# Router on the raw rows, half by half inside the output projection, and the order of splits and slots ahead of the first expert

## What is computed

```python
h = layer_norm(DN_ALPHA * h + y @ w_out, ln1_g, ln1_b)
h = layer_norm(DN_ALPHA * h + moe(h, w_router, b_router, w_gate, w_up, w_down), ln2_g, ln2_b)

def moe(...):                      # 16 experts in 4 groups, 2 chosen of the best group
    scores = sigmoid(h @ w_router)
    sel_score = scores + b_router
    ...
    for e in range(16):
        he = silu(h @ w_gate[e]) * (h @ w_up[e])
        y = y + combine[:, e:e + 1] * (he @ w_down[e])
```

## Time and profile before

| | |
|---|---|
| median of the runs | 886.03 us |
| profiled execution, own time | 888.82 us |
| its span, first to last instruction | 887.1 us |
| TensorE busy | 786.7 us (89%) |
| VectorE busy | 592.4 us (67%) |
| ScalarE busy | 430.9 us (49%) |
| GpSimd busy | 103.2 us (12%) |
| mean granted clock of TensorE | 0.951 of 2.4 GHz |

### The profile page before, as it was taken

One profiled execution on the slowest core, in us unless ns is written; L12 is line 12 of the kernel. 1 busy time (PEld: TensorE's weight loads), 2 busy tenths in 40 slices (PEclk: granted clock), 3 DMA queues, 4 the chain that ended last, 5 costly groups with the idle time before them and its releaser, 6 DMA issues.

```text
span 887.1 us, 10600 instructions
## 1 busy us (share of the span) xinstructions
PE 786.7 (89%) x3903; PEld 617.8 (70%) x3905; DVE 592.4 (67%) x793; ACT 430.9 (49%) x497; POOL 103.2 (12%) x115
## 2 busy tenths in 40 slices
PE   4499999999998999999999984799999999999920
PEld 2387898984676454688788873688888888888710
DVE  4805999793237654222356577799888988898838
ACT  5343343244532644422123121487778777877713
POOL 4630000000001000000000021211112111212012
PEclk9999999997999999999999985899999999999975
DMA  7644132400051300034323975499999999997143
GB/s 187 223 137 157 48 96 57 134 1 1 0 193 60 96 1 0 1 95 159 125 95 104 359 297 177 160 360 384 400 398 397 398 400 396 398 401 272 61 168 136
DMA packets 102644, 167.05 MB, mean 188 GB/s; under 512 B 18961, under 2 KB 39697, under 8 KB 102609
## 3 DMA queue, kind: packets, MB, share of 16 engines
q1 hardware_dynamic: 95024, 145.53, 46.3%
q0 software_dynamic: 4752, 13.11, 3.8%
q10 hardware_dynamic: 2832, 7.93, 2.3%
HBM read 153.38 MB, written 17.40 MB: 193 GB/s over the span
## 4 chain that ended last, share of the span: by engine, by line
PE 77%; DVE 11%; ACT 4%; issue 3%; DMA 2%; SPq 1%; POOL 1%; POOLq 0%; DVEq 0%; ACTq 0%
PE low L1011 14%; PE low L1012 14%; PE low L1013 14%; PE wide L1011 6%; PE wide L1013 6%; PE wide L1012 6%; PE wide L1365 2%; PE low L1188 1%; PE low L1260 1%; PE wide L1173 1%; ACT prob L844 1%; PE wide L1214 1%; PE low L1317 1%; PE low L1252 1%; PE low L1158 1%
## 5 line engine op out<-in xcount | busy, mean ns | idle before, releaser
L1731 DVE TENSOR_TENSOR m_lo<-m_raw,m_hi 128x2048 fp32r<-128x2048 f32 x95 | 214.9, 2290 | 28.4 <-ACT m_hi L890 25.4
L890 ACT ACTIVATE m_hi<-m_raw 128x2048 fp32r<-128x2048 f32 x95 | 179.1, 1917 | 25.6 <-PE low L1013 25.6
L1456 DVE TENSOR_TENSOR w_lo<-raw,w_hi 128x2048 fp32r<-128x2048 f32 x28 | 64.1, 2290 | 79.9 <-ACT w_hi L646 79.6
L1011 PE MATMUL low<-m_hi,xe_hi 128*128 128x512 f32 x256 | 103.7, 405 | 3.6 <-DVE xe_lo L1796 3.2
L1011 PE MATMUL low<-hT_hi,w_hi 128*128 128x512 f32 (+1 forms) x240 | 93.2, 388 | 10.7 <-issue 10.7
L1012 PE MATMUL low<-m_lo,xe_hi 128*128 128x512 f32 x256 | 100.4, 392 | 0.0
L1013 PE MATMUL low<-m_hi,xe_lo 128*128 128x512 f32 x256 | 100.4, 392 | 0.0
L1012 PE MATMUL low<-hT_lo,w_hi 128*128 128x512 f32 (+1 forms) x240 | 93.0, 387 | 0.0
L1013 PE MATMUL low<-hT_hi,w_lo 128*128 128x512 f32 (+1 forms) x240 | 92.3, 385 | 0.0
L646 ACT ACTIVATE w_hi<-raw 128x2048 fp32r<-128x2048 f32 x28 | 53.5, 1910 | 18.6 <-PE wide L1013 8.3
L1011 PEld LDWEIGHTS low<-hT_hi,w_hi 128*128 128x128 f32 x240 | 46.7, 195 | 20.9 <-issue 11.2
(11 more groups left out here) (337 smaller groups left out, 1524.7 us busy)
## 6 DMA issues: line engine op xcount, KB each, us to landing
m_raw<-in_w_gate SPq DMA_DIRECT2D x32, 1024.0 KB, 8.1
m_raw<-in_w_up SPq DMA_DIRECT2D x32, 1024.0 KB, 8.0
m_raw<-in_w_down SPq DMA_DIRECT2D x31, 1024.0 KB, 9.4
raw<-in_w_in SPq DMA_DIRECT2D x19, 1024.0 KB, 5.4
raw<-in_w_out SPq DMA_DIRECT2D x4, 1024.0 KB, 5.1
table_dram<-ftab ACTq DMA_DIRECT2D x8, 328.0 KB, 2.8
strips<-table_dram SPq DMA_DIRECT2D x8, 264.0 KB, 4.2
xn<-in_x SPq DMA_DIRECT2D x4, 512.0 KB, 5.2
```

The lines of the kernel that those rows point to most:

```text
L890: nc.scalar.activation(m_hi[n % MS][:, :], (m_spare if is_last(n, j) else m_raw[slot])[:, :], ACT.Copy).then_inc(q["m_hi_ready"], 1)
L1011: nc.tensor.matmul(outp, lh, rh, start=first, stop=False)
L1456: v.tensor_tensor(w_lo[:, u % SPL, :], raw[:, u % RAW, :], w_hi[:, u % SPL, :].bitcast(F32), ALU.subtract).then_inc(q["lo_ready"], 1)
L1731: v.tensor_tensor(m_lo[n % MS][:, :], (m_spare if is_last(n, j) else m_raw[n % MR])[:, :], m_hi[n % MS][:, :].bitcast(F32), ALU.subtract). ...
```

## The change

The logits of the router are linear in the normalized row but for the row's mean and deviation. So the router is applied to the raw rows (ALPHA·h + y @ w_out) as soon as a half of them is added. Its weights are multiplied by ln1_g and centred over the channels beforehand (`wrc`), so the mean drops out; the logits are then multiplied by `rstd1` and ln1_b's part (`rbias`) is added. The preparation stands early in the kernel: three small loads on SP behind units 0 and 1, four VectorE operations behind `split_lo(1)`, one matmul with ones, two VectorE operations ahead of `split_lo(3)`. Transposes and router are cut into halves of four blocks and put between the parts of half 1 of the output projection; the transposes wait for `z_added`, not for the finished h1, and VectorE waits for the transpose before it centres a row in place. The logits are put together on VectorE in tile 3. Behind the first lists the order of splits and slots changes on VectorE and TensorE.

```diff
@@ SP
             load(0)
             load(1)
+            sp.dma_start(wr[:, :, :], a["w_router"].rearrange("(c p) n -> p c n", p=P)).then_inc(q["wr_loaded"], 16)
+            sp.dma_start(ln1g[:, :], a["ln1_g"][0].rearrange("(c p) -> p c", p=P), allow_slow_non_contiguous=True).then_inc(q["wr_loaded"], 16)
+            sp.dma_start(ln1b[:, :], a["ln1_b"][0].rearrange("(c p) -> p c", p=P), allow_slow_non_contiguous=True).then_inc(q["wr_loaded"], 16)
             for i in range(CONV):
...
-            sp.dma_start(wr[:, :, :], a["w_router"].rearrange("(c p) n -> p c n", p=P)).then_inc(q["late_consts"], 16)
@@ GpSimd
+            step(nc.gpsimd.memset(ones_f[:, :], 1.0))
@@ ScalarE
+            for k in range(TT + 2):
+                turned_out(k)
             store_h1(0)
+            act.wait_ge(q["h1t_used"], 1)
+            nc.scalar.activation(lpart[:, :, :], bank[7][:, 0:TT * NE].rearrange("p (i x) -> p i x", i=TT), ACT.Copy).then_inc(q["part_out"], 1)
             store_h1(1)
-            turned_out(0)
-            turned_out(1)
+            turned_out(TT + 2)
+            store_h1(2)
+            turned_out(TT + 3)
             act.wait_ge(q["z_part"], 4 * TT)
-            store_h1(2)
-            turned_out(2)
             m_split_hi(0)
+            act.wait_ge(q["logit_ready"], 1)
+            nc.scalar.activation(tmp_r[0][:, :, :], logit[:, :, :], ACT.Sigmoid).then_inc(q["scores_ready"], 1)
+            store_h1(3)
             m_split_hi(1)
...
@@ TensorE, early
+            pe.wait_ge(q["wsum_ready"], 1)
+            nc.tensor.matmul(bank[2][:, 480:480 + 2 * NE], ones_f[:, :], wsum[:, :], start=True, stop=True).then_inc(q["wt_done"], 1)
@@ TensorE, output projection
+            def turned(half, i):
+                pe.wait_ge(q["z_added"], 4 * half + i + 1)
+                if half:
+                    pe.wait_ge(q["h1t_out"], i + 3 if i >= 2 else TT)
+                o = bank[4 + i % 2 if half else 4 + i]
+                for c in range(4):
+                    lo = half * 512 + c * P
+                    mm = nc.tensor.transpose(o[:, c * P:(c + 1) * P], h1[:, i, lo:lo + P], ident[:, :])
+                mm.then_inc(q["h1t_done"], 1)
+            def router(half, i):
+                pe.wait_ge(q["h1t_out"], TT + i + 1 if half else TT)
+                o = bank[6 if half else 7][:, i * NE:(i + 1) * NE]
+                for c in range(4):
+                    mm = nc.tensor.matmul(o, hz[:, TT + i % 2 if half else i, c * P:(c + 1) * P], wrc[:, 4 * half + c, :], start=(c == 0), stop=(c == 3))
...
             out_part(1, 0, 0)
             out_part(1, 0, 1)
+            turned(0, 0)
+            turned(0, 1)
             out_part(1, 1, 0)
+            turned(0, 2)
+            turned(0, 3)
             out_part(1, 1, 1)
+            turned(1, 0)
+            router(0, 0)
+            router(0, 1)
             out_part(1, 0, 2)
+            turned(1, 1)
+            router(0, 2)
             out_part(1, 1, 2)
-            turned(0)
-            turned(1)
+            router(0, 3)
+            router(1, 0)
             out_part(1, 0, 3)
+            turned(1, 2)
+            router(1, 1)
             out_part(1, 1, 3)
-            router(0)
-            turned(2)
-            router(1)
-            turned(3)
-            router(2)
-            router(3)
+            router(1, 2)
+            turned(1, 3)
+            router(1, 3)
@@ TensorE, lists
-            lists(2, 8)
             tokens(0, 16)
...
-                if u < 2:
-                    lists(8 + 4 * u, 12 + 4 * u)
+                lists(*((2, 5), (5, 8), (8, 12), (12, 16))[u])
@@ VectorE, early
+            step(v.tensor_tensor(wrc[:, :, :], wr[:, :, :], by_c(ln1g), ALU.mult))
+            step(v.tensor_tensor(wrb[:, :, :], wr[:, :, :], by_c(ln1b), ALU.mult))
+            step(v.tensor_reduce(wsum[:, 0:NE], wrc[:, :, :].rearrange("p c n -> p n c"), AX.X, ALU.add))
+            v.tensor_reduce(wsum[:, NE:2 * NE], wrb[:, :, :].rearrange("p c n -> p n c"), AX.X, ALU.add).then_inc(q["wsum_ready"], 1)
...
+            step(v.scalar_tensor_tensor(out=wrc[:, :, :], in0=bank[2][:, 480:480 + NE].rearrange("p (o n) -> p o n", o=1).to_broadcast([P, KC, NE]),
+                                        scalar=-1.0 / D, in1=wrc[:, :, :], op0=ALU.mult, op1=ALU.add))
+            v.tensor_copy(rbias[:, :], bank[2][:, 480 + NE:480 + 2 * NE]).then_inc(q["widx_ready"], 1)
@@ VectorE, tile i of h1
+                dve.wait_ge(q["h1t_done"], TT + i + 1)
                 step(v.scalar_tensor_tensor(out=h1[:, i, :], in0=h1[:, i, :], scalar=mv1[:, i, 0:1], in1=g1[:, :], op0=ALU.subtract, op1=ALU.mult))
                 dve.wait_ge(q["rstd1_ready"], i + 1)
+                if i == TT - 1:
+                    dve.wait_ge(q["part_out"], 1)
+                    dve.wait_ge(q["router_done"], 1)
+                    step(v.tensor_tensor(logit[:, :, :], bank[6][:, 0:TT * NE].rearrange("p (i x) -> p i x", i=TT), lpart[:, :, :], ALU.add))
+                    step(v.tensor_tensor(logit[:, :, :], logit[:, :, :], rstd1[:, :].rearrange("p (i o) -> p i o", o=1).to_broadcast([P, TT, NE]), ALU.mult))
+                    v.tensor_tensor(logit[:, :, :], logit[:, :, :], rbias[:, :].rearrange("p (o n) -> p o n", o=1).to_broadcast([P, TT, NE]), ALU.add).then_inc(q["logit_ready"], 1)
...
-            for u in range(MS - 1):
-                m_split_lo(u)
@@ VectorE, lists
             slots_of(0, 2)
             lists_out(0, 2)
+            m_split_lo(0)
...
-            slots_of(2, 8)
+            m_split_lo(1)
             m_split_lo(MS - 1)
             xe_lo_out(0)
+            slots_of(2, 8)
+            m_split_lo(3)
             slots_of(8, NE)
...
             lists_out(2, NE)
-            m_split_lo(3)
             m_split_lo(4)
```

More of the change, by code:

```diff
@@ L159, in build @@
         wr = little("wr", [P, KC, NE])
+        rbias = little("rbias", [P, NE])
         A0 = 62.0
@@ L215, in build @@
         yT_lo = at("yT_lo", [P, KC, S], F32R, A0 + 16)
-        h1T = at("h1T", [P, 2, D], F32, 16)
+        hz = at("hz", [P, TT + 2, S], F32, 12)
+        lpart = at("lpart", [P, TT, NE], F32, 8)
+        logit = at("logit", [P, TT, NE], F32, 8.25)
+        wrc = at("wrc", [P, KC, NE], F32, A0 + 144.5)
+        wrb = at("wrb", [P, KC, NE], F32, A0 + 145)
+        ones_f = at("ones_f", [P, P], F32, A0 + 126)
+        ln1g = at("ln1g", [P, KC], F32, A0 + 126.5)
+        ln1b = at("ln1b", [P, KC], F32, A0 + 126.53125)
+        wsum = at("wsum", [P, 2 * NE], F32, A0 + 126.5625)
         g1 = at("g1", [P, D], F32, A0 + 136.5)
@@ L276, in build @@
             z_part h_loaded  vm_ready
-            late_consts z_added var1_ready rstd1_ready h1t_done h1t_used h1t_out h1_ready h1_stored gained
+            late_consts z_added var1_ready rstd1_ready wr_loaded wsum_ready h1t_done h1t_used h1t_out part_out logit_ready h1_ready h1_stored
             router_done scores_ready chosen_ready  dest_ready  listed lists_loaded lists_ready
@@ L895, in store_h1, with turned_out @@
                 act.dma_start(h1_dram[i * P:(i + 1) * P, :], h1[:, i, :]).then_inc(q["h1_stored"], 16)
-            def turned_out(i):
-                act.wait_ge(q["h1t_done"], i + 1)
-                if i >= 2:
-                    act.wait_ge(q["h1t_used"], i - 1)
-                nc.scalar.activation(h1T[:, i % 2, :], wide[i % 2][:, :], ACT.Copy).then_inc(q["h1t_out"], 1)
+            def turned_out(k):
+                act.wait_ge(q["h1t_done"], k + 1)
+                if k >= TT + 2:
+                    act.wait_ge(q["h1t_used"], k - TT)
+                slot = k if k < TT else TT + k % 2
+                nc.scalar.activation(hz[:, slot, :], bank[4 + k if k < TT else 4 + k % 2][:, :], ACT.Copy).then_inc(q["h1t_out"], 1)
+            for k in range(TT + 2):
+                turned_out(k)
             store_h1(0)
+            act.wait_ge(q["h1t_used"], 1)
+            nc.scalar.activation(lpart[:, :, :], bank[7][:, 0:TT * NE].rearrange("p (i x) -> p i x", i=TT), ACT.Copy).then_inc(q["part_out"], 1)
             store_h1(1)
-            turned_out(0)
-            turned_out(1)
+            turned_out(TT + 2)
+            store_h1(2)
+            turned_out(TT + 3)
             act.wait_ge(q["z_part"], 4 * TT)
-            store_h1(2)
-            turned_out(2)
             m_split_hi(0)
+            act.wait_ge(q["logit_ready"], 1)
+            nc.scalar.activation(tmp_r[0][:, :, :], logit[:, :, :], ACT.Sigmoid).then_inc(q["scores_ready"], 1)
+            store_h1(3)
             m_split_hi(1)
-            store_h1(3)
-            turned_out(3)
-            act.wait_ge(q["router_done"], 1)
-            nc.scalar.activation(tmp_r[0][:, :, :], bank[0][:, 0:TT * NE].rearrange("p (i x) -> p i x", i=TT), ACT.Sigmoid).then_inc(q["scores_ready"], 1)
             m_split_hi(MS - 1)
@@ L1118, in _ @@
             index_scores(1)
-            pe.wait_ge(q["widx_ready"], 1)
+            pe.wait_ge(q["widx_ready"], 2)
             for i in range(TT):
```

(21 more changed lines are left out.)

7 lines of the change are left out of this document (4 added, 3 removed).

## The result

The changed kernel takes 893.64 us (median of 4 runs, 893.33 to 894.00); the kernel before, timed beside it on the same chip, 886.35 us. The ratio is 1.0101, interval 1.0067 to 1.0136: slower by 7.3 us, outside the range given (882.5 to 890.3). Repeated later, on another chip, the two gave 891.81 and 886.68, ratio 1.0065 (1.0041 to 1.0089). Four disturbed executions of over 1100 us (one of "before again", one of "reloads held", two of before beside the second group) are in the medians given but not in the ratios.

A forecast was written before the change was run, and what follows sets the result against it. TensorE's unbroken expert loop was taken to pass on any shift of expert 1's first matmul. Start -2.7 plus router and lists +4.1 gave +1.4 on the profiled execution, 887.4 us on the median; range 882.5 to 890.3.

The forecast's parts named there:

- The start: Before TensorE's first product: early loads delay GpSimd, leaving two held VectorE operations instead of four; product 2.7 us earlier.
- A shift of the start arrives whole: From TensorE's first product to the router: no transfer or clock time absorbs an earlier start, so its gain reaches the end.
- The router inside the projection: In the output projection: the idle wait and half-clock router go away, so the selection starts 4.5 us earlier.
- The lists: Selection to expert loop: slower gather (+0.75, +1.3), one long VectorE queue, then half clock on TensorE (+0.9).
- sum of this part and the router: +4.1: Router and lists together: `hidden_out(0)` 3.2 us later plus 0.9 of lost clock; the 4.5 won are more than spent.
- The base: Profiled execution, 0.3% above the median of 886.03 us: the +1.4 worked out on it was put on the median, giving 887.4.
- Case 1: Whole kernel as worked out: 887.4 us, own range 885.4 to 889.2; chance 0.42.
- case 3: At the start: `kvg` comes under 0.8 us later, so nothing is gained; 890.1 us, or 888.6 with 1.5 gained; chance 0.17.
- case 5: Output projection: TensorE's clock falls between transposes and 16-column matmuls, +1.7, 889.1 us; chance 0.07.
- 2: At the start: loads delay GpSimd by over 3 us, one hold or none left, gaining 4.8 to 5.8; 884.8 us; chance 0.17.
- 4: In the lists: gather lands as the first did and no clock is lost, +1.5 instead of +4.1; 884.8 us; chance 0.12.
- 6: Whole kernel: 4.5 us won at the router, list queue hidden, plus the start's 2.7; 878.8 us; chance 0.05.

The follow-up runs named there:

- before again: The kernel before, run once more unchanged: 886.55 us, ratio 1.001.
- reloads held: Changed kernel, but SyncE's expert ring reloads wait until TensorE has turned the first gathered tokens: 890.54 us, ratio 1.0044.
- the second group: List-section follow-ups on the changed kernel: unchanged 891.81 us, reloads waiting for the first tokens 890.54, slots 2 to 7 moved earlier 892.88, these plus later splits 885.11.
- early part only: Kernel before plus the three early loads and the centred router weights and sums, made but not used: 885.56 us, ratio 0.9999.
- mended late: The mended kernel with the chosen experts' weights and overflow places moved behind the last expert: 884.84 us, ratio 0.9992.
- after filled: Changed kernel plus four matmuls without a reader in TensorE's 1.16 us wait near 207 us: 890.25 us, ratio 1.0049.
- filled: Four matmuls without a reader added in TensorE's 1.16 us wait near 207 us: kernel before 882.31 us, changed kernel 890.25.
- the mended kernel: Changed kernel with slots 2 to 7 behind the first lists, split 2 behind `xe_lo`, 3 behind slots 8 to 15, 4 behind `hid`: 885.11 us, ratio 0.9978.

## Why the prediction was wrong, step by step

**The start (-2.7).** Two held operations where four were; first product 36.49 against 37.9. That is the right mechanism, and luck in part. `kvg` was 1.55 us later, but not by three loads of 0.58: they took 1.15, 1.72 and 2.45, and the four `cw` behind them then only 2.85 together, where they had been 6.44. So the seven took 8.3 us where the four had taken 6.4. GpSimd started at 31.14, only 1.07 us later, where the prediction's own line for two holds stood at 31.7. Two it was because VectorE's row stood 0.7 us sooner in this trace (its pair of `hT_lo` at 28.66 instead of 29.40), so that the `hT_lo` at 30.92 got in 0.2 us ahead of GpSimd. Of the thirteen traces with the early loads nine have two holds, three have three (early part only, mended late, after filled) and one has one. In the five traces without the early loads the first product lies at 38.0 to 40.6 (mean 39.3), in the thirteen with them at 33.7 to 39.0 (mean 36.5): 2.8 us. "A shift of the start arrives whole" was wrong. P to Q got 0.8 longer (459.59 against 458.75; filled, 1.4). Followed from one weight split of VectorE to the next, 0.5 us of the gain is lost between those near 67 and 76 us in each of four pairs of traces that I compared (a kernel without the early part and one with it), in the stretch where the change puts its product for the sums and two VectorE operations, which I had called covered. The two products that make `wrc` and `wrb`, priced at 0.28 each, took 2.45 and 2.42 beside GpSimd's work, inside VectorE's long wait. The rest differs from pair to pair: here the clock was half from 69 to 77 us instead of 73 to 77 (1.6 us), and half for 3 us less near 209 to 224. Measured at the end, like for like: 2.0 us for the early part.

**The router inside the projection (-4.5).** Q to S is 4.43 us shorter, the clock stays at 1.00 to the last part, no wait over 0.69: right. What I hadn't seen is that before doesn't always lose what the change saves. In two of six traces with the old router Q to S is 36.8, not 39.2: the half clock at 517 to 520 isn't there. Against these the router's move gives 2.0.

**The lists (+8.6 from S on, with +0.9 of clock in it).** This is the step that failed, in "sum of this part and the router: +4.1". Its mechanisms all show. Its sizes were low, each of them:
- Gather: held +0.94 (I had +0.75, from the row of 2.21). The Trainium skill ("SBUF — State Buffer", section SBUF: two separate sides) would, read strictly, have no two-input VectorE operation hold a descriptor write; the issue took 2.67 us beside a split, 1.67 to 1.73 beside short slot operations. The gather also reads its rows' numbers from SBUF (`now_source`), and no run here tells which of the two was held.
- Its flight beside the reloads: 8.65 - 2.67 = 5.98 against 4.87 - 1.73 = 3.14, so +2.8 where I had taken +1.3 of a bound of 2.9. The bound was the value. Holding the reloads took 2.7 off.
- The wait for split 3: 3.09 (2.9 predicted). S to H in all: +9.55, predicted +7.7; the gather explains 1.7 of that difference.
- TensorE's idle of 6.20 ahead of the hidden transposes (6) and half clock after it, from about 574.6 to 581.4, of which TensorE works from 576.14, 5.3 us. That is past the upper end of my 1.7 to 3.4 us, and the lower end, which I took, stands in no row: both rows that I named show 3.3 to 3.4. E to L is 2.1 longer, less 0.3 in H to E, where I had +0.9. Over the traces of the table E to L is 267.15 to 267.50 where the clock is full behind H and 268.53 to 270.15 where it is half for a while. "Before again" belongs to the second group (268.54), so before loses some of this in some executions as well.
- The end: the last store lands 3.6 us after its issue, not 2.6, as in all kernels with both router and lists changed. Not foreseen.

The step named sized its costs at the middle or the low end, and they came at the dear end. So from S on +12.3, not +8.6: with the router +7.9 instead of +4.1, with the start (-3.3 at Q) +4.6 instead of +1.4 in the trace.

**The base.** The trace of before was an execution with the latest start and with the half clock at 517. I took its distance to the median off as a constant, 2.8 us. But both gains of the change (start, router) were read off exactly what makes that execution long: it lies 1.25 us above the median of before's low-clock executions (887.57). The changed kernel's own trace lay on its median. The rest of the 7.3 comes from the two kinds: the changed kernel's four executions were all of the low clock, and before's median of 886.35 lies between its kinds. Like for like the change costs 5 to 6 us; in the one pair with the fill, 7.9.

**The cases.** Case 1 had the right places and failed by size, case 3 and case 5 failed in mechanism (the start did gain, the clock did not fall in the projection), 2, 4 and 6 were on the wrong side. No case held "each cost of the queue at its upper bound", though every one of them had the same cause, one VectorE queue meeting one transfer.

What stays open: why the last store lands 1.0 us later, with the same bytes moved in the same time; why the clock falls near 210 us in some executions and not in others of one kernel, with the same waits ahead of it. That four products in the wait keep it up in most executions is shown, not why. Which of the mended kernel's moves were needed wasn't tried one by one.

## What to carry to other kernels

When a change removes a wait, look first at what the waiting engine did in it: here two splits of 2.25 us lay in the hole, and the 4.4 us won for the selection were worth nothing until these had found another hole (the gather's flight), for which several moves were made together; the first alone only moved the wait from one line to the next. Bounds that all rest on one mechanism aren't drawn independently: if a transfer collides with what the edit sets free, take the dear end. And before pricing a gain off a single trace, ask whether the thing that is saved is there in every execution; the spread of the runs (884.8 to 887.3 for three, with a trace at 888.8) said that it might not be.

## What the runs showed of the hardware

- TensorE's granted clock differs between executions of one kernel at the same instructions: 0.53 over 209 to 220 us in one trace of the changed kernel, 1.00 in the other, 5.0 us in P to Q. With four products of 0.23 us in a wait of 1.16 us, 42 of 48 executions had a mean clock of 0.954 or more (34 of 36 without the changed kernel, 8 of 12 in it); without them 49 of before's 124, 6 of the mended kernel's 12, 3 of the changed kernel's 14.
- Eleven such products outside that wait kept the clock at 1.00 over 209 to 220 us in before (in the mended kernel only to about 217) and cost 4.7 us: what lies outside a wait is paid for.
- The first gather of 128 rows took 4.8 to 4.9 us from issue to landing on quiet queues, 5.9 with its issue held by a split, and 8.6 to 8.8 (four traces) with 1 MB loads issued beside it as well.
- Small loads on SyncE's queue took 0.58 to 2.45 us to issue by their place behind the large ones, not by their own size: 1.30, 2.01, 2.41, 0.58 for before's four `cw` of 4 KB, and 1.15, 1.72, 2.45 for the changed kernel's router weights (64 KB) and two vectors of 4 KB, with 2.85 for the four `cw` behind them.
